# Output gates through the sigmoid at the projection's read-out, and one comparison per pair to rank the selected blocks, in a hybrid decoder step on one core

## The chip, the cores and the metric

The kernel runs on one core of one Trainium2 chip. The metric is the device time in microseconds (us) of one launch. The time before is the median of three runs.

## The reference

One decoder layer is computed for 512 prompt tokens and for 8 sampled sequences of one new token each (2048 old tokens in a paged cache), with shared weights. Cut to what matters here:

```python
p = (rmsnorm(x) * (1 + sc1) + sh1) @ w_in            # nq, nkv, ng, mqkv, mif, mo, pu
o_nsa = nsa(nq, nkv, ng)                              # compressed, selected and window branches
hm = mlstm(mq, mk * HEAD_DIM ** -0.5, mv, ig, lf)
o_m = sigmoid(mo) * hm                                # the output gate
x = x + gt1 * (concat(o_nsa, o_m, pool_mix(pu)) @ w_out)
x = x + gt2 * conv_ffn(...)
# which blocks of 64 old tokens a sample sees in the selected branch (ns = 33 of them):
forced = (j == 0) | (j == cur) | (j == cur - 1)       # 1e6 instead of the importance
score = where(valid, where(forced, FORCE, imp), -1.0)
top, idx = top_k(score, 16)                           # of equal scores the earlier block
```

For the samples every block is valid, `cur` is block 32, so blocks 0, 31 and 32 are forced, and 13 of the other 30 are chosen by importance.

## The kernel before, in words

Every matrix product is made feature-major: a tile of 128 weight columns is split into a high and a low part (ScalarE makes the high part, `hi`, L1095; GpSimd the low one, L659) and takes 48 matmuls of 260 columns on TensorE (L693). The five engines run five hand-written instruction streams, and semaphores alone order them. A plan (`PART1`, `PART2`) lists the tiles: 21 tiles of the input projection with 16 of the modulation (`ada`), 24 more modulation tiles, then output projection, up and down.

**The projection stage** (`EVENTS_A`). After tile t of the projection, ScalarE copies the PSUM result into `sT` (8 samples, L1168) and `pT` (512 prompt tokens, L1169). Tiles `T_MO` = 12 and 13 hold the output gates `mo`. Between the tiles TensorE scores half a sequence's cached pages (L793, L800), and ScalarE copies those scores out (L1204, L1208) and, for every second half, issues four transfers (L1212).

**The middle stage.** TensorE, VectorE and ScalarE work through the mLSTM of the prompt (16 masked score tiles), window scores and the compressed branch. At its end `head_result(3)` finishes the fourth head (L1595 to L1599), TensorE transposes the heads into PSUM (L938, semaphore `hT_done`), and VectorE multiplies them by the gate into `mix` (L1701) and signals `mmix_ready`. The gate is made just ahead of that as 1 / (1 + exp(-mo)): the exponential on ScalarE (L1298, L1299, `emo_ready`), then an addition (L1697) and a reciprocal (L1698) on VectorE. `mmix_ready` also releases GpSimd, which computes the trailing means (`pool_heads`, L612 to L637), ending with `pool_ready`.

**The samples on VectorE.** Behind `mmix_ready`, in one strict line: sum the importances of a block (`simp`, `sel`), force three blocks, rank (L1717 to L1723), add the mask to the scores (L1725), the maximum (L1726, the third `sx_in`), normalise the compressed probabilities (L1734 to L1741), the products for the sampled mLSTM (L1748 to L1753), scale the probabilities (L1759, `sp_ready`), copy their transposes out of PSUM (L1762, after TensorE's L812 to L818), and the mLSTM state of the samples (L1770 to L1782, `srec_ready`). Ranking compares all 33 x 33 pairs with `is_gt`, all 32 x 32 with `is_equal`, masks the equal ones with the lower triangle `ltri`, adds both and counts.

**The 24 modulation tiles** (`EVENTS_B`) run beside it on TensorE (L706, L776) and ScalarE (L1162, L1147), whose queue also issues the weight loads (L1071), each when the tile six places earlier has been used. Behind the tenth tile ScalarE waits for the third `sx_in` and takes the exponential of the samples' scores (L1223); behind the nineteenth TensorE waits for `sp_ready` (L812).

**The unit loop.** When the modulation tiles, `pool_ready` and VectorE's copies are done, TensorE makes the means' products (L951) and walks through 32 units of prompt attention (`scores` L962, `flip` L977 and L982, `values` L995 and L998); in every fourth unit it also makes `sample_values(b)` for one of the 8 sequences (L1012), which needs that sequence's cached values and window values.

**SyncE's queue.** After `srec_ready` it issues 16 small transfers (L534), four outputs, the cached values of sequences 2 and 3 (L508, 32 transfers), and then `load_window(2)` (L512). It follows that `sample_values(2)` waits, through this queue, for `srec_ready`.

**The rest** is output projection, up, convolution, down and the last norm; TensorE is busy in nearly all of it. There the samples' gate is applied (L1835 to L1838).

Of the kernel before, what the change touches and what calls it, by code (L numbers as in the profile page):

```python
# [20 lines left out]
P = 128  # L21
# [3 lines left out]
NB = 8  # L25
# [12 lines left out]
NSEL = 16  # L38
FF = 2816
# [124 lines left out]
def trunk_kernel(nc, xT, wst, par_d, con_d, hot_d, ltri_d, pt_d, cacheA, cacheV, winK, winV, mC, mst, plst, ffst,  # L164
                 o_y, o_fm, o_vn, o_st, o_snv, o_wk, o_wv, o_C, o_m, o_pool, o_sC, o_sn, o_sm, o_spool, o_ffp, o_ffs):
    with ExitStack() as ctx:
# [94 lines left out]
        rank, simp, sel = lay(0, [NSB * NSB, 136, 4 * 34])  # L261
        sel = sel[0:64, :].rearrange("p (a n) -> p a n", a=4)
        ltri, tie = arena[:, 3120:4144], arena[:, KEEP + 4096:KEEP + 5120]
# [35 lines left out]
        emos = sb("emos", [P, 2, NB])  # L299
# [9 lines left out]
        def par_(name, a=0, b=None, lo=0, hi=P):  # L309
# [51 lines left out]
        num_done, num_evac, hT_done, emo_ready, mmix_ready = (sem("num_done"), sem("num_evac"), sem("hT_done"),  # L361
                                                              sem("emo_ready"), sem("mmix_ready"))
# [697 lines left out]
        def _(act):  # L1060
# [82 lines left out]
            def step(ev):  # L1143
# [6 lines left out]
                if ev[0] == "lin":  # L1150
# [147 lines left out]
            A(emos[:, :, :], sT[:, T_MO:T_MO + 2, :], ACT.Exp, scale=-1.0)  # L1298
            A(dt_[:, :, :], pT[:, T_MO:T_MO + 2, 0:S], ACT.Exp, scale=-1.0).then_inc(emo_ready, 1)  # L1299
# [103 lines left out]
        def _(dve):  # L1403
# [304 lines left out]
            link(V.tensor_reduce(sel[:, 0, 0:NSB], simp[0:64, 0:132].rearrange("p (n r) -> p n r", r=4), AX, ALU.add))  # L1708
            link(V.tensor_tensor(sel[:, 0, 0:NSB], sel[:, 0, 0:NSB], simp[0:64, 4:133:4], ALU.add))
            link(V.memset(sel[:, 0, 0:1], 1e6))  # L1710
# [367 lines left out]
```

## Time and profile before

| | |
|---|---|
| median of 3 runs | 905.02 us (904.6 to 907.04) |
| the profiled execution's own time | 909.6 us |
| its span, first to last instruction | 907.8 us |
| TensorE busy | 831.7 us (92%), 7527 matmuls |
| VectorE busy | 502.9 us (55%) |
| ScalarE busy | 341.9 us (38%) |
| GpSimd busy | 333.0 us (37%) |
| chain that ended last | TensorE 70%, VectorE 14%, SyncE's queue 6%, DMA 3% |
| mean granted TensorE clock | 0.914 of full speed |

All times in the rows further below are microseconds from the start of the span. The chain that ended last is followed backwards from the last instruction: each step is what released the next. TensorE's share of that chain is large, but not where the change lies: between 282 and 371 us it runs mostly over VectorE and SyncE's queue. Time of an engine that is not in the chain costs nothing there.

### The profile page before, as it was taken

Reading aid. Unit: us, or ns where it says so; the run is one execution under the profiler, and the core shown is the slowest. Engines: PE = TensorE matmul, PEld = TensorE weight load, DVE = VectorE, ACT = ScalarE, POOL = GpSimd, SP = SyncE. Lnnn points to the kernel's source line nnn. Section 1 sums busy time; section 2 is a strip of 40 time slices with the busy share of each in tenths; the row PEclk is TensorE's granted clock in tenths of the full one; section 3 lists DMA queues with packets and bytes.
Section 4 is the critical chain, followed back from the end, with each engine's and each line's share of the span. In section 5 each row is a group of like instructions: output and inputs, shape, how many; then the busy total and the mean of one; then the engine's idle time right before and its main releaser. Section 6 shows DMA issues by size and latency. Waiting matters only on the chain.

```text
span 907.8 us, 18995 instructions
## 1 busy us (share of the span) xinstructions
PE 831.7 (92%) x7527; PEld 742.8 (82%) x7527; DVE 502.9 (55%) x971; ACT 341.9 (38%) x650; POOL 333.0 (37%) x201
## 2 busy tenths in 40 slices
PE   2899999998998689899898899999999999999994
PEld 2798998995566456466798899999999999999994
DVE  3724646646348957577445666666421466666224
ACT  4332222223322226456323545555211444555221
POOL 0143545530001964244144134444344444444440
PEclk9999999997556559799899999999999999999997
DMA  9926887861029736443054133333223333222222
GB/s 352 396 90 192 260 265 250 265 226 43 2 71 314 268 112 97 117 116 100 1 215 150 48 99 114 114 116 118 93 94 93 117 113 112 86 92 88 94 65 95
DMA packets 72726, 128.28 MB, mean 141 GB/s; under 512 B 13684, under 2 KB 48444, under 8 KB 72384
## 3 DMA queue, kind: packets, MB, share of 16 engines
q1 hardware_dynamic: 65952, 109.65, 37.8%
q10 hardware_dynamic: 6656, 17.43, 5.8%
q8 instruction: 60, 0.98, 0.5%
q14 instruction: 26, 0.21, 0.1%
q0 software_dynamic: 32, 0.00, 0.0%
HBM read 121.39 MB, written 9.11 MB: 144 GB/s over the span
## 4 chain that ended last, share of the span: by engine, by line
PE 70%; DVE 14%; SPq 6%; DMA 3%; issue 3%; ACT 2%; POOL 1%; DVEq 0%; ACTq 0%
PE ps L693 52%; DMA arena<-cache_keys 2%; PE ps L910 2%; PE ps L925 2%; SPq L508 2%; PE ps L977 2%; PE ps L998 2%; PE ps L962 2%; SPq L457 2%; PE ps L1012 1%; SPq L534 1%; DVE arena L1454 1%; DMA arena<-weights 1%; POOL arena L596 1%; PE ps L899 1%
## 5 line engine op out<-in xcount | busy, mean ns | idle before, releaser
L693 PE MATMUL ps<-hR,wR 128*128 128x260 f32 x3456 | 428.1, 285 | 8.4 <-ACT hR L1103 2.9
L693 PEld LDWEIGHTS ps<-hR,wR 128*128 128x128 f32 x3456 | 421.4, 190 | 13.7 <-issue 5.7
L659 POOL TENSOR_TENSOR wR<-raw,wR 128x1024 fp32r<-128x1024 f32 x92 | 221.8, 2411 | 297.5 <-ACT wR L1095 297.5
L1095 ACT ACTIVATE wR<-raw 128x1024 fp32r<-128x1024 f32 x94 | 99.3, 1058 | 211.2 <-PE ps L693 207.6
L693 PE MATMUL ps<-fR,wR 128*128 128x260 f32 x1056 | 128.1, 283 | 2.2 <-DVE fR L1872 2.0
L693 PEld LDWEIGHTS ps<-fR,wR 128*128 128x128 f32 x1056 | 127.1, 188 | 3.0 <-DVE fR L1872 2.4
L1894 DVE COPY arena<-arena 128x2 f32<-128x2 f32 x44 | 47.6, 1082 | 93.6 <-ACT arena L1380 93.6
L596 POOL TENSOR_TENSOR arena<-arena,par 128x1024 f32<-128x1024 f32 x16 | 34.7, 2169 | 96.8 <-DMA arena<-cache_keys 91.7
L1857 DVE TENSOR_TENSOR t<-ps,mod 128x8 f32<-128x8 f32 x24 | 4.0, 167 | 110.4 <-PE ps L693 110.4
L651 POOL TENSOR_SCALAR arena<-arena,fac 128x128 f32<-128x128 f32 (+3 forms) x32 | 40.7, 1273 | 58.6 <-DVE fac L1811 57.2
L1451 DVE TENSOR_REDUCE arena<-arena 128x64 f32<-128x1024 f32 x16 | 19.5, 1219 | 52.6 <-POOL arena L596 52.6
L1322 ACT ACTIVATE arena<-ps,nmx 128x128 f32<-128x128 f32 (+3 forms) x64 | 33.2, 525 | 14.5 <-DVE nmx L1802 14.0
L1899 DVE SCALAR_TENSOR_TENSOR arena<-arena,par 128x512 f32<-128x512 f32 x44 | 37.1, 843 | 1.6
L1380 ACT ACTIVATE arena<-arena,par 128x520 f32<-128x520 f32 x44 | 36.2, 824 | 1.5
L1315 ACT ACTIVATE arena<-ps 128x256 f32<-128x256 f32 (+3 forms) x32 | 22.5, 704 | 36.3 <-PE ps L982 30.0
L612 POOL MEMSET arena<- 128x15 f32 x2 | 0.2, 108 | 95.1 <-DVE arena L1701 95.1
L1898 DVE SCALAR_TENSOR_TENSOR arena<-arena,par 128x512 f32<-128x512 f32 x44 | 33.1, 752 | 1.6
L1454 DVE TENSOR_TENSOR arena<-arena,par 128x1024 f32<-128x1024 f32 x16 | 33.2, 2073 | 0.0
L977 PEld LDWEIGHTS ps<-con,arena 128*128 128x128 f32 x160 | 17.3, 143 | 15.8 <-issue 11.8
L962 PE MATMUL ps<-arena 64*128 64x128 f32 (+3 forms) x128 | 27.1, 507 | 3.2 <-ACT arena L1322 3.2
L1377 ACT ACTIVATE arena<-ps 128x520 f32<-128x520 f32 x44 | 25.8, 586 | 6.7 <-DVE fR L1872 6.7
L1801 DVE TENSOR_TENSOR ps<-ps,con 128x256 f32<-128x256 f32 x32 | 13.6, 426 | 25.6 <-PE ps L962 25.6
(346 smaller groups left out, 993.7 us busy)
## 6 DMA issues: line engine op xcount, KB each, us to landing
raw<-weights SPq DMA_DIRECT2D x95, 512.0 KB, 3.7
arena<-cache_keys SPq DMA_DIRECT2D x128, 192.0 KB, 3.5
arena<-weights SPq DMA_DIRECT2D x24, 512.0 KB, 10.3
arena<-cache_values SPq DMA_DIRECT2D x128, 64.0 KB, 1.9
arena<-weights ACTq DMA_DIRECT2D x12, 512.0 KB, 5.9
raw<-weights ACTq DMA_DIRECT2D x12, 512.0 KB, 5.1
x<-xT SPq DMA_DIRECT2D x8, 260.0 KB, 4.4
out_y<-x SPq DMA_DIRECT2D x8, 260.0 KB, 2.1
```

The costliest lines, as they stand in the source:

```text
L596: nc.gpsimd.tensor_tensor(tmpv.rearrange("p (a n j) -> p a n j", a=HALF, j=16), pages[:, s, :, 2 * P:3 * P].rearrange("p a (n j) -> p a n ...
L651: nc.gpsimd.tensor_scalar(pr[v % 3][:, 1, 0:(b + 1) * P], pr[v % 3][:, 1, 0:(b + 1) * P], fac[:, v % 2, 1:2], None, ALU.mult)\
L659: nc.gpsimd.tensor_tensor(w_slot(i)[:, 1, :, :], raw[:, g % RAW, :, :], w_slot(i)[:, 0, :, :].bitcast(F32), ALU.subtract).then_inc(lo_read ...
L693: last = mm(ps[:, a + half, 0:TH], w_slot(i)[:, wp, k, :], src[:, hp, j, half * TH:(half + 1) * TH], start=(j == 0 and q == 0), stop=(j == ...
L962: last = mm(ps[:, 2 * (u % 2) + g, 0:n], pT[hr[g], hq, i * P:(i + 1) * P], pT[hr[g], t, 0:n], start=True, stop=True)
L977: last = nc.tensor.transpose(ps[:, 4 + g, c * P:(c + 1) * P], pr[u % 3][:, g, c * P:(c + 1) * P], ident)
L1095: A(w_slot(i)[:, 0, :, :], raw[:, g % RAW, :, :], ACT.Identity).then_inc(hi_ready, 1)
L1322: last = A(pr[k % 3][:, g, 0:n], ps[:, 2 * (k % 2) + g, 0:n], ACT.Exp, bias=nmx[:, k % 2, g:g + 1], accum_out=sm[:, k % 2, g:g + 1])
L1380: A(yab[:, b, :], zb[:, b, 2:T + 2], ACT.Identity, bias=par_("conv_b", t, t + 1), scale=par_("conv_w", 3 * t + 2, 3 * t + 3)).then_inc(y_r ...
L1454: link(V.tensor_tensor(v, v, par_("wpos", 48, 64).unsqueeze(1).unsqueeze(1).broadcast_to([P, HALF, 8, 16]), ALU.mult))
L1894: V.tensor_copy(ffo_p[:, t, :], z[:, S:S + 2])
L1899: last = V.scalar_tensor_tensor(y[:, 0:S], z[:, 0:S], w[0], y[:, 0:S], ALU.mult, ALU.add)
```

## The change

Two edits.

**The gates.** In the projection stage the read-out of tiles 12 and 13 goes through the sigmoid instead of the identity, for samples and prompt. The table set with the sigmoid is loaded before tile 12's read-out and the set with logarithm and exponential after tile 13's. `pT` and `sT` then hold the gates; the exponentials on ScalarE, the additions and reciprocals on VectorE, the buffer `emos` and the semaphore `emo_ready` go away.

**The ranking.** The three forced blocks are left out and 30 candidates stay. One comparison `is_ge` of all 30 x 30 pairs is masked with the strict lower triangle (`below`, a view of `ltri`). Its sums over rows count the earlier candidates that beat a block, its sums over columns the later ones that the block beats; their difference less 1, 2, ... 30 (made by a scan over ones) is the rank shifted by a constant.

```diff
-        rank, simp, sel = lay(0, [NSB * NSB, 136, 4 * 34])
+        rank, simp, sel = lay(0, [NCAND * NCAND, 136, 4 * 32])
+        below = ltri[0:64, :].rearrange("p (j i) -> p j i", i=NSB - 1)[:, 0:NCAND, 1:NCAND + 1]
...
+                    gate = ACT.Sigmoid if T_MO <= t < T_MO + 2 else ACT.Identity
+                    if t == T_MO:
+                        nc.scalar.preload_act_table(ACT.Sigmoid)
                     if t < N_FM:
-                        A(sT[:, t, :], two[:, 1, TH - NB:TH], ACT.Identity, scale=scale)
-                        A(pT[:, t, :].rearrange("p (a n) -> p a n", a=2), two, ACT.Identity, scale=SCALE if t < T_KC else scale)\
+                        A(sT[:, t, :], two[:, 1, TH - NB:TH], gate, scale=scale)
+                        A(pT[:, t, :].rearrange("p (a n) -> p a n", a=2), two, gate, scale=SCALE if t < T_KC else scale)\
                             .then_inc(evac_act, 1)
+                        if t == T_MO + 1:
+                            nc.scalar.preload_act_table_set("natural_log_exp_and_others")
...
-            A(emos[:, :, :], sT[:, T_MO:T_MO + 2, :], ACT.Exp, scale=-1.0)
-            A(dt_[:, :, :], pT[:, T_MO:T_MO + 2, 0:S], ACT.Exp, scale=-1.0).then_inc(emo_ready, 1)
...
-            dve.wait_ge(emo_ready, 1)
-            link(V.tensor_scalar(dt_[:, :, :], dt_[:, :, :], 1.0, None, ALU.add))
-            link(V.reciprocal(dt_[:, :, :], dt_[:, :, :]))
             dve.wait_ge(hT_done, 1)
             windows_moved(dve)
-            V.tensor_tensor(mix[:, 4:6, 0:S], ps[:, 4:6, :], dt_[:, :, :], ALU.mult).then_inc(mmix_ready, 1)
+            V.tensor_tensor(mix[:, 4:6, 0:S], ps[:, 4:6, :], pT[:, T_MO:T_MO + 2, 0:S], ALU.mult).then_inc(mmix_ready, 1)
...
             link(V.memset(simp[0:64, :], 0.0))
+            link(V.memset(sel[:, 2, :], 0.0))
+            link(V.tensor_tensor_scan(sel[:, 3, 0:NCAND], con_("ones", 0, NCAND, 64), con_("ones", 0, NCAND, 64), 0.0, ALU.add, ALU.mult))
...
-            link(V.memset(sel[:, 0, 0:1], 1e6))
-            link(V.memset(sel[:, 0, NSB - 2:NSB], 1e6))
...
-            link(V.tensor_tensor(rk, s_i, s_j, ALU.is_gt))
-            link(V.tensor_tensor(te, s_i[:, 1:, 0:NSB - 1], s_j[:, 1:, 0:NSB - 1], ALU.is_equal))
+            link(V.tensor_tensor(rk, s_i, s_j, ALU.is_ge))
             dve.wait_ge(ltri_landed, 16)
-            link(V.tensor_tensor(tie[0:64, :], tie[0:64, :], ltri[0:64, :], ALU.mult))
-            link(V.tensor_tensor(rk[:, 1:, 0:NSB - 1], rk[:, 1:, 0:NSB - 1], te, ALU.add))
-            link(V.tensor_reduce(sel[:, 1, 0:NSB], rk, AX, ALU.add))
-            link(V.tensor_scalar(sel[:, 2, 0:NSB], sel[:, 1, 0:NSB], float(NSEL) - 0.5, NEG, ALU.is_gt, ALU.mult))
+            link(V.tensor_tensor(rk, rk, below, ALU.mult))
+            link(V.tensor_reduce(sel[:, 0, 0:NCAND], rk, AX, ALU.add))
+            link(V.tensor_reduce(sel[:, 1, 0:NCAND], rk.rearrange("p j i -> p i j"), AX, ALU.add))
+            link(V.tensor_tensor(sel[:, 0, 0:NCAND], sel[:, 0, 0:NCAND], sel[:, 1, 0:NCAND], ALU.subtract))
+            link(V.tensor_tensor(sel[:, 0, 0:NCAND], sel[:, 0, 0:NCAND], sel[:, 3, 0:NCAND], ALU.subtract))
+            link(V.tensor_scalar(sel[:, 2, 1:1 + NCAND], sel[:, 0, 0:NCAND], float(NSEL - NSB) - 0.5, NEG, ALU.is_gt, ALU.mult))
...
-            link(V.tensor_scalar(emos[:, :, :], emos[:, :, :], 1.0, None, ALU.add))
-            link(V.reciprocal(emos[:, :, :], emos[:, :, :]))
             dve.wait_ge(shT_done, 1)
-            V.tensor_tensor(mix[:, 4:6, S:T], ps[:, 7, 0:2 * NB].rearrange("p (t b) -> p t b", t=2), emos[:, :, :], ALU.mult)
+            V.tensor_tensor(mix[:, 4:6, S:T], ps[:, 7, 0:2 * NB].rearrange("p (t b) -> p t b", t=2), sT[:, T_MO:T_MO + 2, :], ALU.mult)
```

On VectorE, from the copy behind the fourth head to the masking of the scores, the order before is (`ps` is PSUM, `arena` the shared buffer in SBUF, partitions x elements of the output, waits in brackets):

```order
L1695 COPY arena<-ps 64x260 [waits num_evac]
L1697 TENSOR_SCALAR arena<-arena 128x1024 [waits emo_ready]
L1698 RECIPROCAL arena<-arena 128x1024 [waits dve_step]
L1701 TENSOR_TENSOR arena<-ps,arena 128x2x512 [waits w_moved,hT_done,dve_step]
...
L1717 TENSOR_TENSOR arena<-arena 64x1089 [waits dve_step]
L1718 TENSOR_TENSOR arena<-arena 64x1024 [waits dve_step]
L1720 TENSOR_TENSOR arena<-arena 64x1024 [waits ltri_landed,dve_step]
L1721 TENSOR_TENSOR arena<-arena 64x32x32 [waits dve_step]
L1722 TENSOR_REDUCE arena<-arena 64x33 [waits dve_step]
```

and in the changed kernel:

```order
L1698 COPY arena<-ps 64x260 [waits num_evac]
L1701 TENSOR_TENSOR arena<-ps,arena 128x2x512 [waits w_moved,hT_done]
...
L1706 MEMSET arena 64x32 [waits dve_step]
L1707 SCALAR_TENSOR_TENSOR arena<-con 64x30 [waits dve_step]
...
L1716 TENSOR_TENSOR arena<-arena 64x900 [waits dve_step]
L1718 TENSOR_TENSOR arena<-arena 64x900 [waits ltri_landed,dve_step]
L1719 TENSOR_REDUCE arena<-arena 64x30 [waits dve_step]
L1720 TENSOR_REDUCE arena<-arena 64x30 [waits dve_step]
L1721 TENSOR_TENSOR arena<-arena 64x30 [waits dve_step]
L1722 TENSOR_TENSOR arena<-arena 64x30 [waits dve_step]
```

The gate's addition and reciprocal are gone; four full-size passes over the pairs and one count became two passes and two counts, with a memset, a scan (L1707) and two subtractions more and two memsets less.

On ScalarE, at the read-outs of tiles 12 and 13 in the projection stage, the changed kernel has:

```order
L1169 ACT_TABLE_LOAD [waits slot_done]
L1171 ACTIVATE sT<-ps 128x8
L1172 ACTIVATE arena<-ps 128x520
L1209 ACTIVATE arena<-ps 128x256 [waits sst_moved0,slc_scored]
L1095 ACTIVATE wR<-raw 128x1024 [waits slot_done,raw_landed0]
L1171 ACTIVATE sT<-ps 128x8 [waits slot_done]
L1172 ACTIVATE arena<-ps 128x520
L1175 ACT_TABLE_LOAD
L1209 ACTIVATE arena<-ps 128x256 [waits slc_scored]
```

Before, the same rows stand there without the two table loads.

## Rows read from the trace of the kernel before

**Rows 1.** The chain that ended last, in time: start, duration, engine and line.
```profile
282.45 6.56 DVE arena L1698
...
329.57 0.77 SPq L534
...
368.17 2.73 DMA arena<-win_values
...
371.03 3.31 PE ps L1012 x46
```

**Rows 2.** Who TensorE waited for, 281 to 372: total, times, longest.
```profile
PE ps L776 <- ACT sq L1162: 8.7, 1, 8.7
PE ps L1012 <- DMA arena<-win_values: 4.3, 1, 4.3
```

**Rows 3.** Timeline of VectorE, gate and ranking: start, duration, line, operation, shapes.
```profile
289.04 1.22 DVE L1701 TENSOR_TENSOR arena<-ps,arena 128x1024 f32<-128x1024 f32 x1
...
291.07 0.21 DVE L1709 TENSOR_TENSOR arena<-arena 64x33 f32<-64x33 f32 x1
...
291.56 1.90 DVE L1717 TENSOR_TENSOR arena<-arena 64x1089 f32<-64x1089 f32 x1
293.49 1.51 DVE L1718 TENSOR_TENSOR arena<-arena 64x1024 f32<-64x1024 f32 x1
295.04 1.97 DVE L1720 TENSOR_TENSOR arena<-arena 64x1024 f32<-64x1024 f32 x1
...
298.59 1.28 DVE L1722 TENSOR_REDUCE arena<-arena 64x33 f32<-64x1089 f32 x1
...
300.11 2.28 DVE L1725 TENSOR_TENSOR arena<-arena 64x2048 f32<-64x2048 f32 x1
```

**Rows 4.** Timeline of VectorE elsewhere: a strided sum, and a product while GpSimd rests.
```profile
6.81 0.37 DVE L1488 TENSOR_REDUCE fold<-con 128x32 f32<-128x128 f32 x1
...
278.02 1.19 DVE L1691 TENSOR_TENSOR arena<-arena,mx 128x992 f32<-128x992 f32 x1
```

**Rows 5.** Timeline of TensorE: the heads' transposes, the means, the last work before `sample_values(2)`.
```profile
281.42 1.97 PE L938 MATMUL ps<-con,arena 128*128 128x128 f32 x8 [1.39 <-DVE arena L1599]
...
330.38 2.05 PE L951 MATMUL ps<-arena,par 128*128 128x512 f32 x2 [0.41 <-ACT mod L1147]
...
366.31 0.44 PE L977 MATMUL ps<-con,arena 128*128 128x128 f32 x2
```

**Rows 6.** Timeline of GpSimd: the trailing means' first and last, one line twice.
```profile
290.38 0.11 POOL L612 MEMSET arena<- 128x15 f32 x1 [95.14 <-DVE arena L1701]
...
300.64 2.84 POOL L629 TENSOR_TENSOR arena<-arena 128x496 f32<-128x496 f32 x1
...
318.64 1.34 POOL L629 TENSOR_TENSOR arena<-arena 128x496 f32<-128x496 f32 x1
...
329.49 0.20 POOL L637 TENSOR_TENSOR arena<-zsum,sT 128x8 f32<-128x8 f32 x1
```

**Rows 7.** Timeline of ScalarE and GpSimd around a weight tile's split, and a table load.
```profile
149.73 1.05 ACT L1095 ACTIVATE wR<-raw 128x1024 fp32r<-128x1024 f32 x1
...
153.09 2.39 POOL L659 TENSOR_TENSOR wR<-raw,wR 128x1024 fp32r<-128x1024 f32 x1
...
512.36 1.28 ACT L1361 ACT_TABLE_LOAD   x1
```

**Rows 8.** Timeline of ScalarE: the exponential of the samples' selected scores.
```profile
304.93 2.01 ACT L1223 ACTIVATE arena<-arena,ssx 64x2056 f32<-64x2056 f32 x1 [8.75 <-DVE ssx L1727]
```

**Rows 9.** Windows: length, five busy times, TensorE's clock, DMA share, GB/s.
```profile
300.00:305.00 5.00, 0.00 (x0) 0.00 (x0) 4.90 (x5) 0.07 (x1) 4.44 (x8) 0.50 0.10 42
310.00:320.00 10.00, 9.59 (x109) 7.00 (x102) 8.53 (x13) 2.63 (x12) 9.43 (x8) 0.50 0.95 332
371.00:376.00 5.00, 4.97 (x56) 3.53 (x58) 0.00 (x0) 0.00 (x0) 0.00 (x0) 0.50 0.38 109
376.00:380.00 4.00, 4.00 (x18) 1.66 (x16) 2.36 (x6) 1.32 (x4) 1.00 (x1) 0.65 0.33 93
```

More of the change, by code:

```diff
@@ L38 @@
 NSEL = 16
+NCAND = NSB - 3
 FF = 2816
@@ L260, in trunk_kernel @@
         swin, ptS = lay(12480 + 17 * T + NB * S, [520, (NPG + ST + 3) * 64])
-        rank, simp, sel = lay(0, [NSB * NSB, 136, 4 * 34])
+        rank, simp, sel = lay(0, [NCAND * NCAND, 136, 4 * 32])
+        ltri = arena[:, 3120:4144]
         sel = sel[0:64, :].rearrange("p (a n) -> p a n", a=4)
-        ltri, tie = arena[:, 3120:4144], arena[:, KEEP + 4096:KEEP + 5120]
+        below = ltri[0:64, :].rearrange("p (j i) -> p j i", i=NSB - 1)[:, 0:NCAND, 1:NCAND + 1]
         so8, vwin = arena[:, KEEP + 6144:KEEP + 7168], arena[:, KEEP + 4096:KEEP + 5120]
@@ L298, in trunk_kernel @@
         strips = [slice(32 * j, 32 * j + 32) for j in range(4)]
-        emos = sb("emos", [P, 2, NB])
         sg = sb("sg", [64, 4])
@@ L360, in trunk_kernel @@
                                                              sem("dt_done"), sem("w_done"))
-        num_done, num_evac, hT_done, emo_ready, mmix_ready = (sem("num_done"), sem("num_evac"), sem("hT_done"),
-                                                              sem("emo_ready"), sem("mmix_ready"))
+        num_done, num_evac, hT_done, mmix_ready = sem("num_done"), sem("num_evac"), sem("hT_done"), sem("mmix_ready")
         rows_moved, saz_ready, sln_ready, sexp_in, sexp_ready, srec_ready = (
@@ L1705, in _ @@
             link(V.memset(simp[0:64, :], 0.0))
+            link(V.memset(sel[:, 2, :], 0.0))
+            link(V.tensor_tensor_scan(sel[:, 3, 0:NCAND], con_("ones", 0, NCAND, 64), con_("ones", 0, NCAND, 64), 0.0, ALU.add, ALU.mult))
             dve.wait_ge(imp_done, 1)
             link(V.tensor_copy(simp[0:64, 1:1 + NCB], ps[0:64, 7, 0:NCB]))
-            link(V.tensor_reduce(sel[:, 0, 0:NSB], simp[0:64, 0:132].rearrange("p (n r) -> p n r", r=4), AX, ALU.add))
-            link(V.tensor_tensor(sel[:, 0, 0:NSB], sel[:, 0, 0:NSB], simp[0:64, 4:133:4], ALU.add))
@@ L1710, in _ @@
-            link(V.memset(sel[:, 0, 0:1], 1e6))
-            link(V.memset(sel[:, 0, NSB - 2:NSB], 1e6))
-            s_i = sel[:, 0, 0:NSB].unsqueeze(1).broadcast_to([64, NSB, NSB])
-            s_j = sel[:, 0, 0:NSB].unsqueeze(2).broadcast_to([64, NSB, NSB])
-            rk = rank[0:64, :].rearrange("p (j i) -> p j i", j=NSB)
-            te = tie[0:64, :].rearrange("p (j i) -> p j i", j=NSB - 1)
-            link(V.tensor_tensor(rk, s_i, s_j, ALU.is_gt))
-            link(V.tensor_tensor(te, s_i[:, 1:, 0:NSB - 1], s_j[:, 1:, 0:NSB - 1], ALU.is_equal))
@@ L1719, in _ @@
-            dve.wait_ge(ltri_landed, 16)
-            link(V.tensor_tensor(tie[0:64, :], tie[0:64, :], ltri[0:64, :], ALU.mult))
-            link(V.tensor_tensor(rk[:, 1:, 0:NSB - 1], rk[:, 1:, 0:NSB - 1], te, ALU.add))
-            link(V.tensor_reduce(sel[:, 1, 0:NSB], rk, AX, ALU.add))
-            link(V.tensor_scalar(sel[:, 2, 0:NSB], sel[:, 1, 0:NSB], float(NSEL) - 0.5, NEG, ALU.is_gt, ALU.mult))
+            link(V.tensor_reduce(sel[:, 0, 0:NCAND], simp[0:64, 4:124].rearrange("p (n r) -> p n r", r=4), AX, ALU.add))
@@ new lines, in _ @@
+            link(V.tensor_tensor(sel[:, 0, 0:NCAND], sel[:, 0, 0:NCAND], simp[0:64, 8:125:4], ALU.add))
+            s_i = sel[:, 0, 0:NCAND].unsqueeze(1).broadcast_to([64, NCAND, NCAND])
+            s_j = sel[:, 0, 0:NCAND].unsqueeze(2).broadcast_to([64, NCAND, NCAND])
+            rk = rank[0:64, :].rearrange("p (j i) -> p j i", j=NCAND)
+            link(V.tensor_tensor(rk, s_i, s_j, ALU.is_ge))
+            dve.wait_ge(ltri_landed, 16)
+            link(V.tensor_tensor(rk, rk, below, ALU.mult))
```

## The prediction

> **What bounds the kernel now.** I read the chain that ended last first, then who TensorE waited for, then the timelines of the engines between 281 and 371 us, and the windows last.
>
> The chain [rows 1] says where the change can act. Over most of the kernel it runs along TensorE, which an edit on VectorE doesn't touch. But from the reciprocal at 282.45 us it lies on VectorE without a break, until SyncE's queue takes over at 329.57 (L534, released by `srec_ready`) and issues one transfer after another until the window load at 368.17; its landing lets `sample_values(2)` start at 371.03. Everything on VectorE from 282 to 329 moves that moment one for one, as long as TensorE gets there early enough. TensorE had ended its last work at 366.75 [rows 5] and then stood idle 4.3 us [rows 2]. After 371 TensorE has work to the end. So the start of `sample_values(2)` is the number to predict.
>
> There are two more waits in the stretch. TensorE stands 8.7 us [rows 2] behind ScalarE, which waits for the third `sx_in` before its exponential at 304.93 [rows 8]; that wait is VectorE's ranking seen from another engine and shifts with it. And GpSimd's trailing means start at 290.38, when `mmix_ready` comes, and end at 329.69 [rows 6], 0.7 us before the products that open the unit loop [rows 5].
>
> **The gates.** Removed on VectorE are an addition and a reciprocal of 128x1024; the reciprocal alone is 6.56 us [rows 1]. What is late next is `hT_done`: the eight transposes run from 281.42 to 283.39 [rows 5]. VectorE is free before that, so the product L1701 starts at about 283.4 instead of 289.04 [rows 3]: **5.6 us** earlier, not the whole of what was removed. ScalarE loses two exponentials at about 275, when it waits for others anyway; I count nothing.
>
> What is added lies in the projection stage: two table loads of 1.28 us [rows 7] (the sigmoid itself replaces an identity of the same size, at the same price by assumption). The first stands ahead of tile 12's read-out, the second behind tile 13's, and at worst each pushes what follows on ScalarE by its whole 1.28 us. TensorE needs a read-out only two tiles later, with 48 matmuls and a half sequence's scores between; what could matter is the split of the next weight tile. Behind the second load ScalarE's part ends at 150.78, and GpSimd takes it up only at 153.09 [rows 7], after the cached pages that it waits for first. 2.3 us of cover against 1.28: cost zero. With the cover gone it would cost up to 1.28 us per load.
>
> The samples' gate at the end of the unit loop loses two instructions of 128x16 that end before the transposed heads are there: zero.
>
> **The ranking.** Before, from the end of L1701 at 290.26 to the masking at 300.11 [rows 3], it is 9.85 us. After, piece by piece:
> - nine small instructions (two memsets, scan, copy, block sums, addition, two subtractions, threshold) at 0.21 us and 0.03 between (L1709 [rows 3]): 2.16;
> - comparison and masking, 900 elements each. The three rows of this kind took 1.90/1089, 1.51/1024 and 1.97/1024 [rows 3], 1.71 ns per element in the mean: 1.54 each and the gaps, 3.14. The same kind took 1.19 us for 992 elements while GpSimd rested [rows 4]; since GpSimd's means will still run beside these two, I take the three nearer rows. Bounds: 1.08 each at 1.2 ns, 1.73 at 1.92 ns;
> - the count over rows, 1.28 x 900/1089 and a gap [rows 3]: 1.09;
> - the count over columns reads with a stride of 30 elements. Its lower bound is the plain count, 1.06. The one strided sum in the trace took 0.37 us for 128 elements [rows 4], which is 2.9 ns per element and 2.6 us for 900 if all of it is rate; but a row of 33 elements takes 0.21 as well, so most of it is fixed. I take 1.4 and a gap, 1.43.
>
> Together 7.8 us, **2.0 us** less. By the bounds the ranking gives back between 0.4 and 3.3.
>
> The Trainium skill (VectorE: DVE Perf Modes, the section on the TRN2 errata) prices an operation from SBUF at 58 cycles plus one per element at 0.96 GHz. That makes 1.0 us of each 900-element pass, and the sum would gain 1.1 us more, 8.7 in all. The row with GpSimd at rest agrees within a tenth; the three rows beside GpSimd do not. The Trainium skill's GPSIMD Engine Reference (what GpSimd shares with VectorE) names instructions with two SBUF inputs as those that collide, and the trace agrees with that.
>
> **The sum.** `sx_in`, `sp_ready` and `srec_ready` come 5.6 + 2.0 = 7.6 us earlier; bounds 6.0 and 8.9. Does it arrive at 371?
> - ScalarE is ready for the exponential from 296.2 (304.93 less its 8.75 idle [rows 8]); it starts at 297.3 instead of 304.93, so TensorE's 8.7 us shrink to about 1.1 and the modulation tiles behind it move by 7.6.
> - The weights: in the hole DMA had fallen to 42 GB/s [rows 9], so that nothing was late when TensorE went on. Then a tile of 512 KB goes every 1.54 us, 340 GB/s, at a DMA share of 0.95 for 332 [rows 9], or 350 GB/s when full. It just keeps up. Zero, but thin.
> - GpSimd starts only 5.6 us earlier, so `pool_ready` moves to 324.1, and becomes what opens the unit loop: 324.2 instead of 330.38, 6.2 us earlier. TensorE gets to `sample_values(2)` at 366.75 - 6.2 = 360.5.
> - SyncE's queue needs 38.6 us from `srec_ready` to the window load [rows 1]: issue at 360.6, start of `sample_values(2)` at 371.03 - 7.6 = 363.4. TensorE is there 2.9 us earlier. The wait shrinks from 4.3 to 2.9, but it remains the bound, and all **7.6 us** arrive.
>
> Against the profiled execution's own 909.6 us that makes 902.0. The median of the runs is 905.0, 4.6 us lower, and I cannot see where that execution lost them; I take the same 7.6 us off the median: **897.4 us**, 0.84% less. About 0.3% (2.7 us) is what a measurement of this kernel can tell from no change.
>
> **The rivals.**
> *The clock stays up.* After the 4.3 us wait TensorE worked at 0.50 of its clock (1.2 instead of 2.4 GHz) from 371 to 376 and at 0.65 in the mean to 380 [rows 9]: 5 x 0.50 + 4 x 0.35 = 3.9 us lost. If the shorter wait of 2.9 us does not bring the clock down, they come on top: 11.5 us, 893.5. For it: less idling. Against it: 2.9 us is still long. 0.15.
> *Weights come late.* The hole of 8.7 us was also DMA's time to catch up. Two window loads of 256 KB that hang on the same `sx_in` now fall into full queues, 1.5 us at 350 GB/s, and twice that if tiles queue behind them. A late tile delays L812, on which VectorE's L1762 and so `srec_ready` hang. The gain is 4.6 to 6.1, about 899.7. 0.12.
> *The wait at 371 isn't there in an ordinary execution.* Then TensorE's own arrival counts, and it moves by 6.2: 898.8. For it: the median is 4.6 us faster than the profile. 0.06.
> *GpSimd takes over.* The means now start beside other VectorE work, and whether the two collide changes a GpSimd instruction from 1.34 to 2.84 us [rows 6]. `pool_ready` opens the unit loop; VectorE's side no longer does. The means took 39.3 us. TensorE reaches 371.03 again when they take 10.5 us longer (371.03 - 360.5); beyond 49.8 us the kernel is slower. If half of them went at the dear price, 0.5 x 39.3 x 1.12 = 22 us, that is 11.5 us too late: 916.5. Against it: the same VectorE instructions in nearly the same order run beside them, with fewer that have two inputs. 0.03.
> *It does less than it says, or gives it back.* The column count is dear and a later wait brings the clock down once more, at 3.9 us: within 0.3% of before. 0.04.
>
> **How the numbers follow.** The forecast as worked out, 896.1 to 899.0 by its bounds, has 0.60. Faster: 0.60 + 0.15 + 0.12 + 0.06 = 0.93; within 0.3%: 0.04; slower: 0.03. The range takes in the first two rivals whole: from 11.5 us and the ranking's upper bound, 892.5, to the loads' lower end of 4.6 us, 900.4, rounded to 900.8.
>
> **What would show it right or wrong.** Right: no VectorE reciprocal of 1024 elements; the product with the gate starts about 0.1 us behind the transposes, near 283.4; 7.8 us from its end to the masking; TensorE's wait behind ScalarE near 1 us; `sample_values(2)` near 363.4, still waiting for the window values; the unit loop opened by GpSimd, no longer by ScalarE; nothing moved between 136 and 200 us. Wrong: a wait for weights among the modulation tiles; the means longer than 41 us; a column count above 2 us; a wait of TensorE for GpSimd's low parts near 155 that is longer than before; or an unchanged start of `sample_values(2)`.

## The result, and the profile after

| | before | with the change |
|---|---|---|
| median, first series | 906.52 us (6 runs, 904.6 to 911.1) | 901.50 us (6 runs, 900.18 to 905.28) |
| ratio to before, first series | | 0.9944 [0.9917, 0.9971] |
| ratio to before, a second series of the same kernel | | 0.995 [0.993, 0.997] |
| the profiled execution's own time, and its span | 909.6, 907.8 us | 905.28, 903.5 us |
| VectorE busy | 502.9 us | 495.5 us |
| mean granted TensorE clock | 0.914 | 0.914 |

The kernel is faster by 5.0 us; 7.6 us were forecast, and 901.5 us lies just above the range.

The gates first: TensorE's transposes of the heads, and VectorE from the product with the gate to the masking, in the timeline of the changed kernel (start, duration, line, operation, shapes; in brackets the idle time before and what ended it).

```profile
285.16 1.97 PE L938 MATMUL ps<-con,arena 128*128 128x128 f32 x8 [1.40 <-DVE arena L1602]
```

```profile
287.17 1.23 DVE L1701 TENSOR_TENSOR arena<-ps,arena 128x1024 f32<-128x1024 f32 x1 [1.61 <-PE ps L938]
288.36 0.17 DVE L1705 MEMSET arena<- 64x136 f32 x1
288.60 0.09 DVE L1706 MEMSET arena<- 64x32 f32 x1
288.72 0.65 DVE L1707 TENSOR_TENSOR_SCAN arena<-con 64x30 f32<-64x30 f32 x1
289.40 0.28 DVE L1709 COPY arena<-ps 64x127 f32<-64x127 f32 x1
289.72 0.27 DVE L1710 TENSOR_REDUCE arena<-arena 64x30 f32<-64x120 f32 x1
290.02 0.48 DVE L1711 TENSOR_TENSOR arena<-arena 64x30 f32<-64x30 f32 x1
290.54 1.52 DVE L1716 TENSOR_TENSOR arena<-arena 64x900 f32<-64x900 f32 x1
292.10 1.84 DVE L1718 TENSOR_TENSOR arena<-arena 64x900 f32<-64x900 f32 x1
293.97 1.08 DVE L1719 TENSOR_REDUCE arena<-arena 64x30 f32<-64x900 f32 x1
295.08 1.84 DVE L1720 TENSOR_REDUCE arena<-arena 64x30 f32<-64x900 f32 x1
296.96 1.04 DVE L1721 TENSOR_TENSOR arena<-arena 64x30 f32<-64x30 f32 x1
298.03 0.22 DVE L1722 TENSOR_TENSOR arena<-arena 64x30 f32<-64x30 f32 x1
298.28 0.17 DVE L1723 TENSOR_SCALAR arena<-arena 64x30 f32<-64x30 f32 x1
298.49 2.29 DVE L1725 TENSOR_TENSOR arena<-arena 64x2048 f32<-64x2048 f32 x1
```

The transposes end at 287.13 and the product starts at 287.17, where it started 5.65 us behind them before [rows 3, 5]. That is the gates' part as forecast. From the product's end (288.40) to the masking (298.49) it is **10.09 us**, where it was 9.85 [rows 3] and 7.8 were forecast. Instructions of 30 elements take between 0.17 and 1.04 us.

The added work in the projection stage, ScalarE's timeline: both table loads take what [rows 7] says, 1.28 us, and each read-out through the sigmoid 0.61 us, where the identity took 0.60 and 0.61 before.

```profile
139.82 1.28 ACT L1169 ACT_TABLE_LOAD   x1 [1.77 <-PE ps L693]
141.11 0.18 ACT L1171 ACTIVATE sT<-ps 128x8 f32<-128x8 f32 x1
141.19 0.61 ACT L1172 ACTIVATE arena<-ps 128x520 f32<-128x520 f32 x1
...
147.96 0.61 ACT L1172 ACTIVATE arena<-ps 128x520 f32<-128x520 f32 x1
148.58 1.28 ACT L1175 ACT_TABLE_LOAD   x1
```

TensorE waited for nobody between 130 and 170 us, and in ten of the eleven kernels below that have the gates' edit it never waited for a low part in the projection stage (in the repeat of the change 0.3 us, and 27 us behind the second load 1.3 us; in the two without the edit 0.6 and 0.4 us). The table loads cost nothing there. Further down, who TensorE waited for between 281 and 371 us (total, times, longest), and its timeline at the two places of [rows 5]:

```profile
PE ps L776 <- ACT sq L1162: 3.8, 1, 3.8
...
PE ps L1012 <- DMA arena<-win_values: 2.3, 1, 2.3
```

```profile
329.72 2.05 PE L951 MATMUL ps<-arena,par 128*128 128x512 f32 x2 [0.41 <-issue]
...
369.80 1.30 PE L1012 MATMUL ps<-arena 128*32 128x128 f32 x40 [2.26 <-DMA arena<-win_values]
```

The wait behind ScalarE has gone from 8.7 to 3.8 us, and the wait for window values from 4.3 to 2.3 [rows 2]. Counted from the start of the transposes, `sample_values(2)` starts 84.64 us later (369.80 - 285.16) instead of 89.61 [rows 5, 1]: 4.97 us gained.

The two profiled executions differ by 4.3 us, but not because of this alone. The windows from 25 to 38 us, which the change does not touch, of the changed kernel and then of the kernel before (start and end, length, five busy times, TensorE's clock, DMA share, GB/s):

```profile
25.00:30.00 5.00, 3.88 (x28) 3.15 (x21) 3.33 (x5) 2.70 (x4) 0.00 (x0) 0.50 1.02 406
30.00:38.00 8.00, 8.00 (x87) 7.27 (x85) 3.88 (x11) 1.60 (x3) 0.00 (x0) 0.51 1.04 396
```

```profile
25.00:30.00 5.00, 4.37 (x58) 3.78 (x50) 3.42 (x5) 2.79 (x4) 0.00 (x0) 0.78 1.03 409
30.00:38.00 8.00, 7.86 (x117) 7.35 (x119) 5.14 (x18) 2.42 (x5) 0.00 (x0) 1.00 1.03 395
```

TensorE was granted 1.2 GHz for 13 us there. The read-out of tile 11, ahead of all that the change touches, is already 3.2 us late (131.61 against 128.40), and the transposes of L938 start at 285.16 instead of 281.42. So: 3.7 us lost early, 5.0 gained in between, and 3.1 gained behind 370 us, where the clock stayed at 1.00 this time (L1012's 40 matmuls 1.30 us, 2.36 before). Start of L938 varies from 280.1 to 287.3 us over the profiled executions below. **I therefore measure every trace from L938 on**, and compare times by ratios alone.

### The profile page after: what moved, and what is told of

It reads as the page before. It is cut to its first block, busy times and chain, and to the rows that moved or that the text cites. A ratio compares the mean times of both kernels' runs of the same rounds, so it can differ in the third digit from the quotient of the medians.

```text
span 903.5 us, 18991 instructions
## 1 busy us (share of the span) xinstructions
PE 833.7 (92%) x7527; PEld 744.6 (82%) x7527; DVE 495.5 (55%) x968; ACT 343.7 (38%) x650; POOL 328.9 (36%) x201
## 4 chain that ended last, share of the span: by engine, by line
PE 77%; DVE 11%; SPq 5%; ACT 2%; issue 2%; DMA 2%; POOL 1%; DVEq 0%; ACTq 0%; POOLq 0%
PE ps L693 57%; PE ps L910 2%; PE ps L925 2%; SPq L508 2%; PE ps L977 2%; PE ps L998 2%; PE ps L962 2%; PE ps L800 1%; PE ps L1012 1%; SPq L534 1%; DMA arena<-weights 1%; PE ps L899 1%; PE ps L793 1%; PE ps L875 1%; PE ps L717 1%
## 5 line engine op out<-in xcount | busy, mean ns | idle before, releaser
L1802 DVE TENSOR_REDUCE nmx<-ps 128x2 f32<-128x256 f32 (+3 forms) x32 | 26.4, 825 | 1.1
```

## The experiments

Two distances are read from each trace. The *block* is from the product's end to the masking. The *stage* is from the start of the transposes (L938) to the start of the means' products (L951), which open the unit loop. Times of before over all series have medians of 906.5 to 908.2 us. The ratios compare runs of the same series, and are not the quotients of two medians of this table.

| kernel | block | stage | gained in the stage | wait for window values, longest | median, ratio to before [95%] |
|---|---|---|---|---|---|
| before | 9.85 | 48.96 | | 4.3 | |
| the change | 10.09 | 44.56 | 4.4 | 2.3 | 901.50, 0.9944 [0.9917, 0.9971] |
| the change, again | 10.07 | 44.52 | 4.4 | 1.7 | 904.35, 0.995 [0.993, 0.997] |
| gates only | 9.84 | 43.36 | 5.6 | 2.5 | 901.37, 0.9927 [0.9899, 0.9955] |
| ranking only | 10.08 | 50.12 | -1.2 | 3.0 | 911.26, 1.0038 [1.0015, 1.006] |
| change, means later | 7.31 | 49.25 | -0.3 | 0 | 905.46, 0.9976 [0.9957, 0.9994] |
| gates only, means later | 7.88 | 49.83 | -0.9 | 0 | 904.38, one run |
| change, scan ahead | 8.30 | 41.85 | 7.1 | 0 | 898.92, 0.9912 [0.9887, 0.9938] |
| change, page loads ahead of the state rows | 10.07 | 44.51 | 4.5 | 2.5 | 900.86, 0.994 [0.9913, 0.9966] |
| gates only, page loads ahead | 9.85 | 43.37 | 5.6 | 8.8 | 907.71, 0.9996 [0.9969, 1.0024] |
| change, window load earlier | 10.08 | 44.50 | 4.5 | 2.8 | 903.42, 0.9957 [0.9931, 0.9983] |
| scan ahead, window load earlier | 8.30 | 41.86 | 7.1 | 0 | 899.57, 0.9905 [0.9867, 0.9943] |
| gates only, window load earlier | 9.84 | 43.34 | 5.6 | 3.0 | 900.88, 0.9923 [0.9898, 0.9949] |

**1. Each part alone.** Gates only keeps the ranking of before:

```diff
-            link(V.tensor_scalar(dt_[:, :, :], dt_[:, :, :], 1.0, None, ALU.add))
-            link(V.reciprocal(dt_[:, :, :], dt_[:, :, :]))
...
-            V.tensor_tensor(mix[:, 4:6, 0:S], ps[:, 4:6, :], dt_[:, :, :], ALU.mult).then_inc(mmix_ready, 1)
+            V.tensor_tensor(mix[:, 4:6, 0:S], ps[:, 4:6, :], pT[:, T_MO:T_MO + 2, 0:S], ALU.mult).then_inc(mmix_ready, 1)
```

Ranking only is the other half of the diff on the gates of before.

> The gates' part alone; the ranking is that of before. Theory A (the gates brought the whole gain, the ranking none): the product with the gate again starts within 0.1 us of the end of the heads' transposes instead of 5.65 us behind it, the stretch from the product's end to the masking stays at 9.9 us, and the time is that of the full change within 1.5 us, some 5 us below before. Rival B (the ranking brought its 2 us and something else lost them): this kernel is about 2 us slower than the full change, 3 us below before.

> The ranking's part alone; the gates are made with exponential and reciprocal as before. Theory A: from the end of the product with the gate to the masking of the scores it takes 9.5 to 10.5 us as in the full change, and the time is that of before within 1.5 us. Rival B: 7.8 us for that stretch and a time 2 us below before; the 10.1 us in the full change would then be an accident of how GpSimd's means lie beside it.

> The full change itself once more, for a second trace and on the same chip as the parts. If the stretch before 135 us, which the change does not touch, was 3.8 us longer in the first trace by accident of the clock (0.50 of full speed from 25 to 38 us), this trace shows the third head result at another time, and the wait before sample_values(2) and the clock behind it may differ too. Expected: product with the gate within 0.1 us of the transposes' end, product to masking 9.5 to 10.5 us, time 5 us below before.

The gates bring 5.6 us in the stage and 0.73% in time: all of the gain, and by the stage 1.2 us more than the whole change (the intervals of the two times overlap). The ranking alone makes the stage 1.2 us longer and the kernel slower, by 0.38% [0.15, 0.60], which is 1.4 to 5.4 us. Its trace shows more of that behind the stage: counted from L938, `sample_values(2)` starts 1.8 us later than before (91.37 against 89.61) and the next one 2.5 us later (106.89 against 104.41). The forecast's 2.0 us for the ranking is refuted in sign.

**2. GpSimd out of the way.** The means wait for the third `sx_in` instead of `mmix_ready`, first with the new ranking, then with the old:

```diff
-                    pool.wait_ge(mmix_ready, 1)
+                    pool.wait_ge(sx_in, 3)
```

> The full change, but GpSimd's trailing means are released by the third sx_in (after the ranking, the masking and the maximum) instead of by the product with the gate, so that GpSimd rests while VectorE ranks. Theory A1 (VectorE's instructions with two SBUF inputs, small ones too, wait for GpSimd): the stretch from the product to the masking falls from 10.1 to about 7 us: small instructions of 0.1 to 0.3 us, the two passes over 900 elements 1.1 us each. Rival A2 (the new instructions are dear in themselves): it stays within 0.7 us of 10.1. For the column sum, 1.84 us again says that its stride is dear, 1.1 us that it was GpSimd. Time: the means end near 330 us instead of 323.8, which takes back what VectorE gains, so the full change's time within 2 us by either.

> The gates' part with the ranking of before, and GpSimd's means put behind the ranking (the wait for the projected scores in place of mmix_ready), as in the run of the full change with later means, where the new ranking took 7.3 us. Theory E: the old ranking falls as well, by what its three two-input passes and small instructions lose to GpSimd, from 9.84 us to under 9.3 us, and the difference between the old and the new ranking with GpSimd at rest is the 2.0 us of the forecast, give or take 0.4. Rival F (GpSimd has nothing to do with it; the means' place changes something else): the old ranking stays at 9.8 us.

VectorE in the run of the new ranking with the means later, the same instructions as above:

```profile
283.69 0.21 DVE L1707 TENSOR_TENSOR_SCAN arena<-con 64x30 f32<-64x30 f32 x1
...
284.56 0.20 DVE L1711 TENSOR_TENSOR arena<-arena 64x30 f32<-64x30 f32 x1
284.80 1.09 DVE L1716 TENSOR_TENSOR arena<-arena 64x900 f32<-64x900 f32 x1
285.92 1.09 DVE L1718 TENSOR_TENSOR arena<-arena 64x900 f32<-64x900 f32 x1
287.04 1.08 DVE L1719 TENSOR_REDUCE arena<-arena 64x30 f32<-64x900 f32 x1
288.16 1.84 DVE L1720 TENSOR_REDUCE arena<-arena 64x30 f32<-64x900 f32 x1
290.03 0.18 DVE L1721 TENSOR_TENSOR arena<-arena 64x30 f32<-64x30 f32 x1
```

GpSimd does nothing from the product to the masking in this run (its means start at 295.58, its work before them had ended 105 us earlier), and every instruction with two inputs falls: the scan from 0.65 to 0.21, the addition from 0.48 to 0.20, the passes from 1.52 and 1.84 to 1.09, the subtraction from 1.04 to 0.18. The Trainium skill (VectorE: DVE Perf Modes, the section on the TRN2 errata) has a formula for an addition of N elements, (N + 151) / 0.96 ns, which gives 1.09 us for 900 and 0.19 us for 30; the trace agrees. The prediction had quoted the table of the same section, which gives 1.0 us for 900. Both sums stay as they were: the one over columns costs **1.84 us whether GpSimd works or not**, 1.7 times the sum over rows. With GpSimd at rest the new ranking takes 7.31 and the old 7.88 us. So with GpSimd at rest the new one is worth 0.57 us, not the 2.0 that the second expectation still had; beside GpSimd it loses 2.8 us and the old one 2.0. One of the old one's four passes, with GpSimd at rest (beside GpSimd 1.51 [rows 3]):

```profile
287.38 1.22 DVE L1717 TENSOR_TENSOR arena<-arena 64x1024 f32<-64x1024 f32 x1
```

How the loss comes about is seen when GpSimd's timeline of the changed kernel is laid beside VectorE's rows above:

```profile
288.69 0.61 POOL L614 COPY arena<-arena 128x512 f32<-128x512 f32 x1
289.38 1.06 POOL L622 TENSOR_TENSOR arena<-arena 128x526 f32<-128x526 f32 x1
290.51 0.60 POOL L620 COPY arena<-arena 64x512 f32<-64x512 f32 x1
291.19 1.79 POOL L622 TENSOR_TENSOR arena<-arena 64x524 f32<-64x524 f32 x1
293.05 1.36 POOL L624 COPY arena<-arena 64x512 f32<-64x512 f32 x1
...
296.72 1.23 POOL L629 TENSOR_TENSOR arena<-arena 128x496 f32<-128x496 f32 x1
```

The scan starts 0.03 us behind GpSimd's copy (288.72 against 288.69) and ends 0.07 behind its end (289.37 against 289.30). The addition L1711 ends at 290.50, GpSimd's sum at 290.44. The subtraction L1721 starts at 296.96 inside GpSimd's 296.72 to 297.95 and ends at 298.00. It works in the other direction too: GpSimd's copy L624 starts inside L1718, which ends at 293.94, and takes 1.36 us instead of 0.60. The Trainium skill (SBUF — State Buffer, the section on who interferes with whom) says that a VectorE instruction with two SBUF inputs and a GpSimd instruction that reads SBUF block each other for the whole instruction, whoever starts first, and that sums are left alone. These rows agree on both points: of the two that overlap the later one ends late, on either engine, and the sum over rows takes 1.08 us beside GpSimd and without it. A small two-input instruction therefore costs, in these rows, what is left of the GpSimd instruction that it meets.

The kernels themselves did not gain over the change (0.9976 against 0.995): here GpSimd's means end at 329.23, and TensorE waited for them at the unit loop's opening:

```profile
PE ps L951 <- POOL arena L637: 8.9, 1, 8.9
```

That is the forecast's rival "GpSimd takes over", made by hand: the means are off the path only while they start early.

**3. The scan out of the way.** In the changed kernel VectorE idles 1.61 us ahead of the product. The two memsets and the scan depend on nothing there:

```diff
+            link(V.memset(simp[0:64, :], 0.0))
+            link(V.memset(sel[:, 2, :], 0.0))
+            link(V.tensor_tensor_scan(sel[:, 3, 0:NCAND], ...))
             dve.wait_ge(hT_done, 1)
...
-            link(V.memset(simp[0:64, :], 0.0))
-            link(V.memset(sel[:, 2, :], 0.0))
-            link(V.tensor_tensor_scan(sel[:, 3, 0:NCAND], ...))
```

> The full change with its two memsets and the scan moved ahead of VectorE's wait for hT_done, into the 1.6 us in which VectorE idles there; GpSimd is between its pieces then. Theory E (the small two-input instructions are dear only because they meet GpSimd's means): the scan takes 0.2 us there, not 0.65, the product still starts at 0.04 us behind the transposes, and the block from the product's end to the masking falls from 10.1 to about 9.1 us; the time falls by about 0.9 us, which is 0.999 of the changed kernel and at the bound of what can be told. Rival F (their price is that of the second reading of PSUM or of the link from one to the next, not of GpSimd): the scan takes 0.65 us wherever it stands, and the instruction that now comes first beside GpSimd, the copy out of PSUM, rises instead; the block falls by the 0.9 us less what the next ones rise.

VectorE, from the scan on:

```profile
282.24 0.21 DVE L1701 TENSOR_TENSOR_SCAN arena<-con 64x30 f32<-64x30 f32 x1
283.57 1.23 DVE L1704 TENSOR_TENSOR arena<-ps,arena 128x1024 f32<-128x1024 f32 x1 [1.12 <-PE ps L938]
...
285.32 0.44 DVE L1711 TENSOR_TENSOR arena<-arena 64x30 f32<-64x30 f32 x1
285.79 2.00 DVE L1716 TENSOR_TENSOR arena<-arena 64x900 f32<-64x900 f32 x1
287.82 1.38 DVE L1718 TENSOR_TENSOR arena<-arena 64x900 f32<-64x900 f32 x1
...
292.25 0.18 DVE L1721 TENSOR_TENSOR arena<-arena 64x30 f32<-64x30 f32 x1
```

The scan costs 0.21 us ahead of the product, as theory E says. The block falls by 1.8 us, not 0.9: 1.0 is what was moved, with its gaps, and 0.86 is the subtraction L1721, which now meets no long instruction of GpSimd and takes 0.18 instead of 1.04. Behind the block the same happens again (`sx_in` to `sp_ready` 13.96 us, 14.94 in the changed kernel, 13.98 before), so that the stage is 2.7 us shorter than the changed kernel's. Theory E was right in kind and short in size; the expected 0.9 us was only what was moved. Where the later instructions fall among GpSimd's is not under control here: the two passes took 2.00 and 1.38 us, 3.38 together, as much as in the changed kernel (3.36) and shared out otherwise. The time agrees with the stage: 0.9912, and 0.9905 in the kernel of experiment 5.

**4. SyncE's order, first attempt.** Two kernels, the full change and gates only, try to take the wait for window values away. SyncE issues the page loads of examples 2 and 3 ahead of the state rows:

```diff
             load_window(1)
+            sp.wait_ge(pool_ready, 1)
+            sp.wait_ge(early_out, 16 * 5)
+            load_values(2)
+            load_values(3)
             sp.wait_ge(srec_ready, 1)
```

> The full change, and on SyncE the loads of the values for examples 2 and 3 issued ahead of the wait for srec_ready (behind the wait for pool_ready, which guards the buffers) and of the state stores behind it. It leaves VectorE's work as it is. Theory A (the value products of example 2 hang on srec_ready only through SyncE's queue, and this is how the gates' gain got to the end): TensorE's wait for window values at the first sample_values(2), 2.3 us in the changed kernel's profile, is under 0.3 us, and the time falls by those 2.3 us, to about 0.9975 of the changed kernel, 0.992 of the kernel before; the values' loads land some 4 us earlier. Rival B (the values wait for the weight transfers that take their share of the DMA engines then, not for SyncE's place in line): the wait stays over 1.5 us, and the time is that of the changed kernel within 1 us. Rival C (the loads, put earlier, delay the move of the state rows that srec_ready releases, and the wait goes to those rows' readers): the wait for values goes, and the time stays or rises.

> The gates' part alone with the ranking of before, and SyncE's loads of values 2 and 3 ahead of its wait for srec_ready. Theory A: the 2.5 us wait that was left in the gates-only kernel goes too, and since nothing else that is late hangs on srec_ready in this stretch, this kernel gains these 2.5 us over the gates-only kernel: ratio to the kernel before about 0.990. It also says that with this order the ranking's price (1.1 us on srec_ready's chain) is no longer seen, so that this kernel and the full change with the same order differ by under 1 us. Rival D (the ranking costs its time elsewhere, in the unit loop's opening or by the clock): this kernel is 2 us or more faster than the full change with the same order.

Theory A falls. The wait stays at 2.5 us in one kernel and grows to 8.8 in the other. In the first the numbers are those of rival B, but the load that is waited for is not the one that either had in mind. The chain of waits of the first, around that wait:

```profile
353.17 0.65 SPq L544
353.87 11.86 DMA arena<-win_values
365.86 1.81 PE ps L1013 x46
```

and the same stretch in the changed kernel:

```profile
366.76 2.90 DMA arena<-win_values
```

TensorE waits for the window load, not for the pages; I had moved the wrong loads. The window load is now issued 8.7 us earlier, counted from L938 (353.87 - 280.93 against 366.76 - 285.16), but it lands after 11.9 us instead of 2.9. Right ahead of it in the queue stand the state rows and the stores. In the changed kernel 32 page issues stood between, and DMA was 0.72 busy for 43 GB/s from 345 to 350 us, long before the window load. Here it is 0.89 busy for 49 GB/s just behind the issue:

```profile
355.00:360.00 5.00, 5.00 (x56) 3.79 (x56) 3.54 (x13) 3.21 (x9) 1.39 (x2) 1.00 0.89 49
```

So the rows and stores are what most likely holds the load up; no run moved them alone. In the gates-only kernel it is issued at 359.45 and takes 11.0 us, which makes the wait of 8.8. The issue is 4.4 us later than in the other kernel, counted from L938, because the page loads now wait for `pool_ready`, and the means take 39.3 us beside the old ranking and 35.2 beside the new one. The 5.6 us of the gates are all given back (0.9996).

**5. SyncE's order, second attempt.** Only the window load itself is moved, between the page loads of examples 2 and 3, in three kernels:

```diff
             load_values(2)
+            sp.wait_ge(spv_done, 1)
+            load_window(2)
             load_values(3)
...
-                sp.wait_ge(spv_done, b - 1)
-                load_window(b)
+                if b > 2:
+                    sp.wait_ge(spv_done, b - 1)
+                    load_window(b)
```

> The full change, and on SyncE the load of the window of values for example 2 issued between the page loads of example 2 and those of example 3 (behind its own wait, that the products of example 0 are done), not behind both. In the run with both page loads moved ahead of the state rows the wait stayed, since the window's own load still came last. Theory G (TensorE's wait at the third sample product is for this one load, which stands behind 16 issues of the state rows, 4 stores and 32 page issues, 38 us after srec_ready): the load is issued some 11 us earlier, near 355 us, the wait of 2.3 us goes, and the time falls by 2 us or a little more: 0.997 to 0.998 of the changed kernel, about 0.992 of the kernel before. Rival H (the pages of example 3 or the clock set the start next): the wait goes and the time stays within 1 us of the changed kernel's.

> Scan and memsets ahead of the product, as in the run before, and the window's load between the page loads. Theory G: the kernel with the scan ahead had no wait for window values in its profile, so there is nothing left for the earlier load to take: the time is that of the kernel with the scan ahead, 0.991 of the kernel before, within 1 us. It also tells whether that kernel's 0.991 comes again: the block from the product's end to the masking is 8.3 us again. Rival H (what the scan's place gave was chance of the clock): the ratio is back at 0.994 to 0.995, though the block is 8.3 us.

> The gates' part alone, with the ranking of before, and the window's load between the page loads. Theory G: its profile had a wait of 2.5 us for that load and 2.4 us for the slow clock behind it; the wait goes, and the time falls by 2.5 us or more from the gates-only kernel's 0.9927: about 0.990. Against the full change with the same load earlier this kernel is 1.1 us faster, the price of the new ranking on the chain (hT to srec_ready 42.5 against 43.6 us); a difference of 3 us or more says that the ranking costs something that the chain does not show.

In the full change the load is issued 10.5 us earlier, counted from L938 (353.21 - 282.08), and `sample_values(2)` no longer waits. But the next one does:

```profile
376.87 1.30 PE L1015 MATMUL ps<-arena 128*32 128x128 f32 x40 [2.82 <-DMA arena<-win_values]
```

Its window load now stands behind 32 page issues of about 0.65 us each, and is issued at 373.96: the chain of waits runs over SyncE's issues without a break from 353.21 on. The wait is SyncE's issue rate, and it moved on by one example; the times stay those of the same kernels without this edit. Gates only has the same wait, 3.0 us, and 0.9923 instead of the expected 0.990. Neither theory G nor H foresaw it. The two kernels with the scan ahead have no such wait with either order, and the same time, as the expectation for the second said.

## Why the forecast was off

*"The gates: 5.6 us."* Right to a tenth of a microsecond: 5.60 in the stage of the gates-only kernel. TensorE did not wait for the table loads, as argued. Outside the stage there is a small difference: from tile 11's read-out to L938 nine of the eleven profiled executions with the gates' edit take 153.5 to 153.8 us (the others 152.8 and 155.0), and the two without it 152.9 and 153.0. In the nine the granted clock falls to 1.2 GHz 83 to 84 us behind that read-out, in the other four 85 to 87 us behind it. Whether the edit causes the earlier fall, no run shows.

*"Nine small instructions at 0.21 us and 0.03 between: 2.16."* **This step failed.** They took 3.67 us: scan 0.65, addition 0.48 and subtraction 1.04 are over 0.21 by 1.5 us together, and each ends with a GpSimd instruction. The row for 0.21 was an addition that had met only the last tenth of a microsecond of a copy (GpSimd's, 290.56 to 291.17; the addition starts at 291.07). I named the collision of two-input instructions and applied it to the long passes alone.

*"Comparison and masking: 3.14."* 3.43 beside GpSimd. Three rows beside GpSimd were the right source, and the error is only 0.3.

*"The count over columns: 1.43."* Measured 1.88 with its gap, and 1.87 with GpSimd at rest. The upper bound of 2.6 and the lower of 1.06 held it; the value that I took did not.

The count over rows was 0.02 over its 1.09. Together that makes 7.82 + 1.51 + 0.29 + 0.45 + 0.02 = 10.09, the whole of the block. The comparison with the block of before (9.85) was also lopsided: the old one's four two-input passes were taken from rows that already held GpSimd's delays, the new small ones from rows that held none. The runs with GpSimd at rest say what the edit is worth in itself, 0.57 us.

*"`sx_in`, `sp_ready` and `srec_ready` come 7.6 us earlier."* Counted from L938 they came 5.4, 4.4 and 4.5 us earlier: 5.6 from the gates, less 0.24 in the block, less 0.95 between `sx_in` and `sp_ready`, where the line-up with GpSimd had shifted too. There L1728 took 0.85 us (0.27 before and in the kernel with the scan ahead) and the pair L1734 3.00 (1.38 in both), and later instructions won part of that back (L1741 1.24 instead of 2.07). Rows of the changed kernel:

```profile
303.20 0.85 DVE L1728 TENSOR_SCALAR scm<-scm,sg 64x127 f32<-64x127 f32 x1
304.08 3.00 DVE L1734 TENSOR_TENSOR arena<-arena,con 128x496 f32<-128x496 f32 x2
```

TensorE's wait behind ScalarE shrank to 3.8 us, not to the forecast's 1.1.

*"It remains the bound, and all arrive."* Right: `sample_values(2)` still waits for the window values, 2.3 us (2.9 forecast). Of the 4.5 us of `srec_ready` all arrive there, with 0.5 more, since SyncE's queue took 37.9 us and not 38.6. By the ratios the time gained 5.0 us and the repeat 4.5 (the repeat's medians are 2.7 us apart), against 4.4 in the stage. In ten of the eleven series with an interval, the stage's gain lies in the ratio's interval or within a microsecond of it; the intervals are 3 to 7 us wide, so this is no sharp test. The eleventh is the kernel with the wait of 8.8 us, and that wait is 6.3 us longer than in the gates-only kernel.

*"GpSimd becomes what opens the unit loop, 324.2."* Wrong: the means ended at 323.75, 6 us ahead of L951. They took 35.2 us, not 39.3: that goes with the new ranking beside them (35.2 in five profiled executions with it, 39.3 in four with the old, 37.8 with the scan ahead, 33.7 when the means start behind either ranking). And the ranking's part that was to bring VectorE ahead of them did not come. TensorE's last modulation tiles, behind L812 and so behind `sp_ready`, opened it.

*The rivals.* Had "the clock stays up" decided, the kernel would be faster than forecast. It did stay up in the profiled execution, where 3.1 us were gained behind 370, and not in the repeat, where L1012 took 2.01 us. Weights came late for 1.0 us in all in the changed kernel, for 1.3 before. None of the rivals decided it: the sum itself was too large by 3.1 us, of which the range had allowed 1.6 for the ranking.

**What stays open.** The ranking alone costs 1.4 to 5.4 us in time and 1.2 in the stage. From L938 to its end its one profiled execution is 2.5 us longer than that of before; whether the rest of the median's 3.4 us is chance, the runs do not say. Nor do they say why both profiled executions of the changed kernel, and none of its variants, ran TensorE so slowly from 25 to 50 us (mean granted clock 0.70; 0.80 to 0.98 in the others). The best kernel measured is the change with the scan ahead of the product: 0.9912 [0.9887, 0.9938], a gain of 8.0 us by the ratio. Its interval overlaps that of the change, but a second kernel with the same edit gave 0.9905. Gates with the old ranking come next, at 0.9927 and 0.9923.

## What to carry to other kernels

Where two engines block each other, do not price a small two-input instruction by its size: it costs up to the whole of the other engine's instruction under way, here 0.2 to 1.0 us for 30 elements. Here 2.0 us were forecast for fewer elements, and collisions of three small instructions took 1.5 of them. Put what depends on nothing into the wait that an earlier gain has opened. And before a queue is reordered, ask which of its loads is waited for, what would then stand ahead of it in the queue, and whether the queue's issue rate will bring the same wait back one step later.

## What the runs showed of the hardware that was not expected

- VectorE's sum over 900 elements takes 1.08 us along the rows and 1.84 us with a stride of 30 elements, beside GpSimd and with GpSimd at rest.
- The copy of 64x127 out of PSUM took 0.27 or 0.28 us and the sum over rows 1.08 us, beside GpSimd and without it.
- A load of 256 KB landed after 2.9 us behind page loads and after 11.0 and 11.9 us right behind 16 small state rows and the state stores of the same queue.
- Moving three small instructions changed another one nine microseconds later by 0.86 us, by where it fell among GpSimd's.
- After idling 2.3 and 2.5 us TensorE went on at 2.4 GHz (40 matmuls 1.30 us), and after 2.5 us in another kernel at 1.2 GHz (2.36 us).
